# Attention weights of one head in two turned by VectorE and the DMA queues instead of TensorE

## The reference, cut to what matters

```python
z = jnp.einsum('bhqd,bhkd->bhqk', qb, kb) * scale          # strictly causal, 128 queries at a time
log_keep = jnp.where(mask, jax.nn.log_sigmoid(-z), 0.0)
suffix = lax.cumsum(shifted, axis=3, reverse=True)         # shifted: log_keep moved by one
A = jnp.where(mask, jnp.exp(jax.nn.log_sigmoid(z) + suffix), 0.0)
outs.append(jnp.einsum('bhqk,bhkd->bhqd', A, vb).astype(v.dtype))
```

## Time and profile before

| | |
|---|---|
| time, median of 3 runs | 1184.14 us (1182.91 to 1186.34) |
| the profiled execution's own time | 1188.73 us |
| span in its profile | 1186.7 us |
| PE busy over the span | 1113.4 us (94%) |
| DVE busy | 885.8 us (75%) |
| ACT busy | 730.3 us (62%) |
| attention units 0 to 27 with projection | about 116 to 416 us |
| attention units 28 to 31 | about 416 to 437 us |

### The profile page before, as it was taken

The page is one execution under the profiler, slowest core; times in us unless marked ns, Lnnn a source line. Parts: engine busy times, 40 slices in busy tenths (PEclk is TensorE's granted clock), DMA queues, the critical chain, the costliest instruction groups (busy, mean ns, idle before and its releaser), DMA issues. The chain is left out here.

```text
span 1186.7 us, 16929 instructions
## 1 busy us (share of the span) xinstructions
PE 1113.4 (94%) x5868; PEld 910.8 (77%) x5868; DVE 885.8 (75%) x1013; ACT 730.3 (62%) x914; POOL 136.3 (11%) x192
## 2 busy tenths in 40 slices
PE   8998999999999989997799999999999999999960
PEld 7886877877778758886688888888888888888840
DVE  4405656667575573467699999999999999999957
ACT  5422654656743582122588888888888888888840
POOL 1001000010010011010101111111111111111000
PEclk9999999999999989998899999999999999999995
DMA  7111001101011055002899999999999999999619
GB/s 233 39 36 36 19 18 37 36 19 36 19 36 37 1 213 195 36 36 101 351 428 405 393 394 380 394 384 378 392 379 381 385 380 378 383 386 385 241 69 380
DMA packets 59835, 261.90 MB, mean 221 GB/s; under 512 B 14224, under 2 KB 36240, under 8 KB 46608
## 3 DMA queue, kind: packets, MB, share of 16 engines
q1 hardware_dynamic: 48992, 240.32, 52.8%
q0 software_dynamic: 9216, 16.80, 3.7%
q10 hardware_dynamic: 1584, 4.20, 0.9%
HBM read 252.89 MB, written 25.17 MB: 234 GB/s over the span
## 5 line engine op out<-in xcount | busy, mean ns | idle before, releaser
L1132 DVE TENSOR_TENSOR e_lo<-W,e_hi 128x1024 fp32r<-128x1024 f32 x384 | 452.6, 1219 | 25.8 <-ACT e_hi L1126 22.9
L1126 ACT ACTIVATE e_hi<-W 128x1024 fp32r<-128x1024 f32 x384 | 403.4, 1060 | 97.0 <-PE ps L1097 97.0
L1095 PE MATMUL ps<-e_hi,xT_hi 128*128 128x512 f32 x512 | 204.5, 399 | 4.5 <-DVE e_lo L1132 3.5
L1097 PE MATMUL ps<-e_lo,xT_hi 128*128 128x512 f32 x512 | 201.6, 394 | 0.0
L1096 PE MATMUL ps<-e_hi,xT_lo 128*128 128x512 f32 x512 | 201.0, 393 | 0.0
L847 DVE TENSOR_TENSOR_SCAN kept<-kept,start_at 128x1024 f32<-128x1024 f32 (+7 forms) x64 | 89.4, 1397 | 57.8 <-ACT kept L653 57.7
L433 PE MATMUL ps<-xnT_hi,w_hi 128*128 128x512 f32 x320 | 128.8, 403 | 2.4 <-DVE y_mix L822 0.9
L433 PE MATMUL ps<-xnT_hi,w_lo 128*128 128x512 f32 x320 | 128.2, 401 | 0.0
L433 PE MATMUL ps<-xnT_lo,w_hi 128*128 128x512 f32 x320 | 125.2, 391 | 0.0
L1095 PEld LDWEIGHTS ps<-e_hi,xT_hi 128*128 128x128 f32 x512 | 97.7, 191 | 24.1 <-DVE e_lo L1132 3.7
L662 ACT ACTIVATE probsT<-ps 128x512 f32<-128x512 f32 (+3 forms) x96 | 43.7, 490 | 113.9 <-PE ps L482 113.8
(11 more groups left out here) (234 smaller groups left out, 1692.2 us busy)
## 6 DMA issues: line engine op xcount, KB each, us to landing
W<-in_w_dram SPq DMA_DIRECT2D x96, 2048.0 KB, 11.2
w_raw<-in_w_in_dram SPq DMA_DIRECT2D x20, 512.0 KB, 4.0
yy<-y_rows SPq DMA_DIRECT2D x7, 1024.0 KB, 12.0
xt<-in_x_dram SPq DMA_DIRECT2D x8, 512.0 KB, 3.8
w_out_raw<-in_w_out_dram SPq DMA_DIRECT2D x8, 512.0 KB, 7.4
xn_rows<-xn SPq DMA_DIRECT2D x8, 512.0 KB, 2.6
out_dram<-x ACTq DMA_DIRECT2D x7, 512.0 KB, 8.4
x<-in_x_dram SPq DMA_DIRECT2D x2, 1536.0 KB, 10.1
```

The lines of the kernel that those rows point to most:

```text
L1095: pe.matmul(o, xs_hi[:, k], e_hi[:, p, cols], start=(k == 0), stop=False)
L1097: mm = pe.matmul(o, xs_hi[:, k], e_lo[:, p, cols], start=False, stop=(k == last))
L1126: act.activation(e_hi[:, p], flat[:, p * D:(p + 1) * D], ACT.Copy).then_inc(s["hi_made"], 1)
L1132: dve.tensor_tensor(e_lo[:, p], flat[:, p * D:(p + 1) * D], e_hi[:, p], ALU.subtract).then_inc(s["lo_made"], 1)
```

## The change

For head 0 of each pair the unit's `soft` is no longer turned by PE. Instead DVE transposes it in 32x32 blocks within each group of 32 partitions, into a row of `y_mix` that is free at that time. SP writes this row to DRAM (`spread`, one transfer of 128 rows), waits for it, and reads it back in four transfers of 32 partitions each (`collect`), which puts the blocks where a full transpose would have them, in `probsT[0]`. `values` waits for these reads (`exchanged`) as well. Head 1 is turned by PE and copied by ACT as before. `th` counts head 1's PSUM blocks alone. ACT's `open_unit` for head 0 waits for the DVE transpose instead of PE's. The loads of `w_raw` and `w_out_raw` now stand between the new transfers.

```diff
+            def spread(n):
+                sp.wait_ge(quads_made, n + 1)
+                sp.dma_start(quads(n), quads_turned(n).rearrange("p b k i -> p (b k i)")).then_inc(spread_out, 16)
+
+            def collect(n):
+                sp.wait_ge(spread_out, 16 * (n + 1))
+                if n:
+                    sp.wait_ge(valued, n)
+                for b in range(QUADS):
+                    sp.dma_start(quads_home(n)[b * QUAD:(b + 1) * QUAD].rearrange("j a k i -> j a (k i)"),
+                                 quads(n).rearrange("(a j) (b r) -> b j a r", a=QUADS, b=QUADS)[b]).then_inc(exchanged, 16)
...
+            for n in range(LIGHT):
+                spread(n)
+                if n:
+                    for part in range(2):
+                        for g in groups_in(n - 1, part):
+                            if g % 2 and g // 2 + 2 < len(CHUNKS):
+                                load_chunk(g // 2 + 2)
+                collect(n)
+            for n in range(LIGHT, UNITS):
+                spread(n)
+                if n == LIGHT:
+                    sp.wait_ge(filled, 2 * len(CHUNKS))
+                for c in OUT_ORDER[2 * (n - LIGHT):2 * (n - LIGHT) + 2]:
+                    sp.dma_start(w_out_raw[:, c], w_out_v[:, c]).then_inc(w_out_in[c], 16)
+                collect(n)
...
-                turn(n, 0)
                 project(ticks_by(n, 0), ticks_by(n, 1))
-                turn(n, 1)
+                turn(n)
...
-                if n:
-                    act.wait_ge(turned, th(n - 1, h) + halves(n - 1))
+                if n and h:
+                    act.wait_ge(turned, th(n))
+                elif n:
+                    act.wait_ge(quads_made, n)
...
                 for h in range(2):
-                    take_turned(n, h)
+                    if h:
+                        take_turned(n)
...
                 dve.tensor_tensor(s[:, :L - 1], s[:, :L - 1], k[:, 1:], ALU.mult).then_inc(weighed, 1)
+                if h:
+                    return
+                if n:
+                    dve.wait_ge(spread_out, 16 * n)
+                dve.wait_ge(weighed, 2 * n + 1)
+                dve.transpose(quads_turned(n).rearrange("p b k i -> p k b i"), s.rearrange("p (k b i) -> p k b i", b=QUADS, i=QUAD)).then_inc(quads_made, 1)
```

More of the change, by code:

```diff
@@ L77, in hymba_moe_layer @@
     y_rows = nc.dram_tensor("y_rows", (PAIRS, D), F32, kind="Internal").ap()
+    quad_rows = nc.dram_tensor("quad_rows", (2, P * S), F32, kind="Internal").ap()
     with ExitStack() as ctx:
@@ L220, in hymba_moe_layer @@
         rows_squared = sem("rows_squared")
-        rows_logged = sem("rows_logged")
         rows_inverse = sem("rows_inverse")
@@ L231, in hymba_moe_layer @@
         turned_read = sem("turned_read")
+        quads_made = sem("quads_made")
+        spread_out = sem("spread_out")
+        exchanged = sem("exchanged")
         valued = sem("valued")
@@ L292, in hymba_moe_layer, with quads_turned, quads, quads_home @@
         assert all(z_first[n] % 2 == 0 for n in range(UNITS) if halves(n) == 2)
-        th = lambda n, h: sum(2 * halves(m) for m in range(n)) + h * halves(n)
+        th = lambda n: sum(halves(m) for m in range(n))
+        QUAD = 32
+        QUADS = P // QUAD
+        def quads_turned(n):
+            return y_mix[:, CB + n // NT, 0:length(n)].rearrange("p (b k i) -> p b k i", b=QUADS, i=QUAD)
+        def quads(n):
+            L = length(n)
+            return quad_rows[n % 2, 0:P * L].rearrange("(p c) -> p c", c=L)
+        def quads_home(n):
+            return probsT[0].rearrange("p k t -> p (k t)")[:, 0:length(n)].rearrange("p (a k i) -> p a k i", a=QUADS, i=QUAD)
         TB = lambda g: ps[:, 4 + g % 2]
@@ L339, in mix_sp @@
                     sp.dma_start(router_b[:, NG:], b_expert.partition_broadcast(P)[:, 0, :]).then_inc(router_in, 16)
-            for c in range(2, len(CHUNKS)):
-                load_chunk(c)
-            sp.wait_ge(filled, 2 * len(CHUNKS))
-            for c in OUT_ORDER:
-                sp.dma_start(w_out_raw[:, c], w_out_v[:, c]).then_inc(w_out_in[c], 16)
+            def spread(n):
[8 more added lines that the diff above has]
+                                 quads(n).rearrange("(a j) (b r) -> b j a r", a=QUADS, b=QUADS)[b]).then_inc(exchanged, 16)
+            for c in range(2, PRE + 2):
+                load_chunk(c)
+            for n in range(LIGHT):
[13 more added lines that the diff above has]
+                collect(n)
         def mix_pool(pool):
@@ L473, in scores, with turn @@
                 mm.then_inc(scored, 1)
-            def turn(n, h):
+            def turn(n):
+                h = 1
                 pe.wait_ge(weighed, 2 * n + h + 1)
                 for hf in range(halves(n)):
-                    g = th(n, h) + hf
+                    g = th(n) + hf
                     if g >= 2:
@@ L487, in values @@
                 p, t = n // NT, tile_of(n)
-                pe.wait_ge(turned_read, th(n + 1, 0))
+                pe.wait_ge(turned_read, th(n + 1))
+                pe.wait_ge(exchanged, 16 * QUADS * (n + 1))
                 if n == 0:
@@ L495, in values @@
                         head = slice((2 * p + h) * HD, (2 * p + h + 1) * HD)
-                        mm = pe.matmul(ps[h * HD:(h + 1) * HD, VB, (t % 4) * P:(t % 4 + 1) * P], v[:, j, head], probsT[h][:, j, :],
+                        mm = pe.matmul(ps[h * HD:(h + 1) * HD, VB, (t % 4) * P:(t % 4 + 1) * P], v[:, j, head], probsT[1][:, j, :] if h else quads_home(n)[:, :, j],
                                        start=(j == 0), stop=(j == t))
@@ L542, in mix_pe @@
                     scores(n + 1)
-                for h in range(2):
-                    turn(n, h)
+                turn(n)
                 if n == UNITS - 3:
@@ L559, in mix_pe @@
             pe.wait_ge(end_squared, 3)
-            pe.wait_ge(turned_read, th(UNITS, 0))
+            pe.wait_ge(turned_read, th(UNITS))
             pe.matmul(ps[:, 4], same_head, last_sq[:, 0:BANK], start=True, stop=True).then_inc(end_summed, 1)
@@ L654, in open_unit, with take_turned @@
                 act.activation(soft[h][:, S - L:S - 1], z[:, 0:L - 1], ACT.Sigmoid, scale=up).then_inc(z_read, halves(n))
-            def take_turned(n, h):
+            def take_turned(n):
+                h = 1
                 for hf in range(halves(n)):
-                    act.wait_ge(turned, th(n, h) + hf + 1)
+                    act.wait_ge(turned, th(n) + hf + 1)
                     if hf == 0 and n:
@@ L661, in take_turned @@
                     k0, k1 = 4 * hf, min(4 * hf + 4, length(n) // P)
-                    act.activation(probsT[h][:, k0:k1, :], TB(th(n, h) + hf)[:, 0:(k1 - k0) * P].rearrange("p (k t) -> p k t", t=P),
+                    act.activation(probsT[h][:, k0:k1, :], TB(th(n) + hf)[:, 0:(k1 - k0) * P].rearrange("p (k t) -> p k t", t=P),
                                    ACT.Copy).then_inc(turned_read, 1)
```

3 lines of the change are left out of this document (removed).

## The result

The changed kernel takes 1189.0 us (median of 6 runs, 1187.25 to 1190.13), the kernel before 1184.95 us (median of 6, 1182.91 to 1186.34). The ratio is 1.0034, with a 95% interval of 1.0024 to 1.0044: 4 us slower, where 5.4 us of gain were forecast.

A forecast was written before the change was run, and what follows sets the result against it. PE's issue time was taken to bound units 0 to 27, a chain through ACT and DVE units 28 to 31. 9.9 - 1.3 - 3 x 0.25 - 2.4 = 5.4 us gained: 1178.7 us, 8-in-10 range 1173 to 1190.

The forecast's parts named there:

- PE would stand about 2.1 us there: At units 8, 16 and 24, PE idles about 2.1 us until DVE has read the projection bank.
- PE's clock falls in the new stalls: Rival, 8 in 100: PE drops to 1.2 GHz behind four new stalls, 3 us each, 12 us in all; 1190.7 us.
- All other units to 27: Units up to 27 except 0, 8, 16, 24: PE saves head 0's transposes at 0.10 us each, 9.9 us gained.
- Unit 0, 1.3 us lost: At unit 0, DVE's transpose delays head 1's multiply and PE's transposes behind it; 1.3 us lost.
- Units 8, 16, 24, 0.25 us each: At these pair starts PE follows DVE's later bank read, and its saved transposes become waiting; 0.25 us lost each.
- DVE's transpose, 1.22 us: The added DVE transpose takes the multiply's time, 1.22 us at 1024 columns and 0.29 us at 128.
- the rival of the scan's rate: Rival, 14 in 100: DVE's transpose runs at the scan's rate, 1.17 us more at each of four places; 1183.4 us.
- The exchange, c = 4.5 us, hidden to unit 27: A unit's exchange reads take 4.5 us; the projection's 24 matmuls cover them through unit 27.
- The exchange binds the last four units: Rival, 16 in 100: reads cost 7.0 us, making the chain in units 28 to 31 12.8 us longer; 1189.1 us.
- Units 28 to 31, 2.4 us lost: Without projection cover, four serial reads lengthen the chain 2.8 us; waits at the end take up 0.4; 2.4 us lost.
- the clock is 0.50 behind the new stalls: A listed sign that the prediction is wrong: PE at its 1.2 GHz level after the new stalls.

The follow-up runs named there:

- transposes_alone_filled: Kernel before plus unused DVE transposes of head 0 in units 0 to 27, no exchange, with 12 dummy PE transposes at units 8, 16, 24; 1191.42 us.
- other_head_late_transposes: Against the changed kernel: head 1 exchanged, PE turns head 0, DVE transposes later in units 0, 8, 16, 24, units 28 to 31 turned by PE; 1234.34 us.
- transposes_alone: Kernel before, both heads turned by PE, plus DVE transposes of head 0 in units 0 to 27, result unused, no exchange; 1194.23 us.

## Why the prediction was wrong, step by step

The step that failed is the one that let the new stalls cost their length alone. "PE would stand about 2.1 us there" was right (2.05), but the sum gave "PE's clock falls in the new stalls" nothing, and the rival 8 in 100. It is what happened: 12 falls in 15 at units 8, 16 and 24 over five traces, and low windows behind unit 0's stall in all five. The rival's size was off too: it took 3 us for a fall, from the one behind 3.19 us. At the three starts a fall cost 1.6 us, and even the one behind 3.19 us is worth 2.0 against the trace that has none. At a mean of 12 / 15 x 3 falls of 1.6 us, plus unit 0's 2.1, that is 3.8 + 2.1 = 5.9 us, more than the whole forecast gain.

The other terms, each against the ledger:

- *All other units to 27, 9.9 us.* Measured 2.52 + 2.01 + 2.05 + 1.54 = 8.1. Between the marks 0 and 7 lie 28 of head 0's transposes (the forecast's 27 and unit 7's one), so a transpose taken off is worth 0.090 us, not 0.10 (2.52 / 28), and in units 14 and 22 DVE's extra load makes PE wait 0.65 us, where it had not waited.
- *Unit 0, 1.3 us lost.* 1.04 to 1.24 in four traces with the clock held: right.
- *Units 8, 16, 24, 0.25 us each.* 0.36 to 0.41 with the clock held: right in kind, 0.4 us more in all.
- *DVE's transpose, 1.22 us.* 1.25 at 1024 columns; the rival of the scan's rate is out. The Trainium skill's 311 ns for a 128x128 block in bf16 (VectorE: DVE Perf Modes, The three transpose paths) is met by this f32 one at 128 columns, but 1024 take four times that, not eight:

```profile
L900 DVE STREAM_TRANSPOSE y_mix<-soft 128x1024 f32<-128x1024 f32 x4 | 5.0, 1245 | 0.3
...
L900 DVE STREAM_TRANSPOSE y_mix<-soft 128x128 f32<-128x128 f32 x4 | 1.2, 312 | 0.4
```

- *The exchange, c = 4.5 us, hidden to unit 27.* Hidden, yes, and c is 4.4 to 4.75. So "The exchange binds the last four units" did not come true at its 7.0 us.
- *Units 28 to 31, 2.4 us lost.* The chain itself was priced well: 18.8 us became 22.0 (416.33 to 438.36) for 4 x 4.5 + 3.5 = 21.5, and the 0.4 us that the end was to absorb did not come back. But the 18.8 held some 6 us of low clock behind the 3.19 us stall, and five of the seven other traces with PE's transposes there have less of it or none, so against the mean the loss is about 4.1 us.

Put together: 8.1 - 1.2 - 1.2 - 4.1 = 1.6 us of gain without the falls at the four starts, less 5.9 us for them, makes 4.3 us slower; 4.05 was measured.

The forecast's own list of what would show it wrong named "the clock is 0.50 behind the new stalls". The evidence ahead of the run was two points, 0.66 us with no fall and 3.19 us with one. Stalls of 2.1 to 2.5 us lay between, four of them. The argument gave them the clock of the shorter, at odds of more than ten to one, with nothing in the rows to carry such odds. That the exchange rival's number, 1189.1, is the measured one is chance: its mechanism, reads of 7.0 us, is not what happened. The Trainium skill (TensorE: Matmul & The Clock Gate, Part 1) also says that when the gate acts varies from run to run against the kernel's start. The two executions of one program above agree, and a single profile could not have shown it.

A version that beats both kernels came of it: the exchange in the 24 units where projection covers it and DVE is not waited for, PE's transposes in units 0, 8, 16, 24 and 28 to 31, 1173.64 us, 11.4 us under the kernel before.

## What to carry to other kernels

Price a new PE stall with the clock's fall behind it, or run both cases as equals; at the starts here a stall of 2 us cost 0.4 us net without the fall and 2.0 with it. Where work is moved off the busy engine, move it in the units where that engine is the bound and leave it where another engine is already waited for: which units were in the set decided between 4 us slower and 11 us faster. If a stall can't be removed, idle work in it may hold the clock.

## What the runs showed of the hardware

- A PE stall of 2.05 us was followed by the 1.2 GHz level in 12 of 15 cases, and one of 1.99 us in 2 of 3; the stalls of 0.64 to 0.67 us in units 8, 14, 16, 22 and 24 never were. Each of these falls cost 1.6 us; behind unit 0's stalls of 2.50 to 3.57 us, all five followed by it, 1.3 to 2.9 us.
- Length alone did not decide it: no fall followed a stall of 2.34 us (transposes_alone_filled, unit 0), nor one of 2.98 us (other_head_late_transposes, 280.52), nor, in one of eight traces, the stall of 3.2 us ahead of unit 28's values (transposes_alone, 430.86).
- With PE at work through most of the same waits, every window behind them read 1.00, with the exchange in the program and without it.
- 0.13 to 1.0 MB more of DMA traffic per unit (87 instead of 28 GB/s over eight units) changed no step of the ledger by more than 0.06 us. But a 64 to 128 KB write issued right behind 1 MB of loads landed in 4.2 to 4.3 us instead of 2.2 to 2.4.
